# Dilated keys of a sample batch held once, new keys in the near tiles, page numbers read ahead

## The reference

```
for win, dil in DIL_CONFIGS:
    j = jnp.arange(win // dil + 1)
    idx = n_buf + jnp.arange(Tn)[:, None] - j[None] * dil
    g = kv_all[:, jnp.maximum(idx, 0)]
    s = jnp.einsum('bqhd,bqjhd->bhqj', q, g[:, :, :, 0]).astype(jnp.float32) * SCALE
    s = s - slopes[:, None, None] * (j * dil).astype(jnp.float32)
    p, lse = _masked_softmax(s, idx >= 0)
    outs.append(jnp.einsum('bhqj,bqjhd->bqhd', p.astype(q.dtype), g[:, :, :, 1]))
    lses.append(jnp.transpose(lse, (0, 2, 1)))
return _combine_dilations(outs, lses)
```

## Time and profile before

| | |
|---|---|
| median of 3 runs | 2328.37 us (2328.33 to 2331.82) |
| profiled execution | 2330.11 us, span 2328.2 us, mean granted TensorE clock 0.994 |
| TensorE matmul busy | 2238.4 us, 96% of the span |
| TensorE weight load busy | 1599.4 us, 69% |
| VectorE, ScalarE, GpSimd busy | 897.8 (39%), 566.9 (24%), 646.7 us (28%) |
| chain that ended last | PE 89%, DVE 4%, issue 4% |
| DMA | 448.19 MB, 193 GB/s on average |
| DMA's busy share, 465 to 582 us | 0.82 at 292 GB/s |

### The profile page before, as it was taken

The page is one execution under the profiler, slowest core; times in us unless marked ns, Lnnn a source line. Parts: engine busy times, 40 slices in busy tenths (PEclk is TensorE's granted clock), DMA queues, the critical chain, the costliest instruction groups (busy, mean ns, idle before and its releaser), DMA issues.

```text
span 2328.2 us, 43538 instructions
## 1 busy us (share of the span) xinstructions
PE 2238.4 (96%) x13592; PEld 1599.4 (69%) x13592; DVE 897.8 (39%) x2384; ACT 566.9 (24%) x1356; POOL 646.7 (28%) x719
## 2 busy tenths in 40 slices
PE   7999999999999999999999999999999899999998
PEld 4545567676766777777745455777676677777776
DVE  2013754343344222336510157434344522233374
ACT  2102651111123412220211046311111233221202
POOL 0002760101043443444100047410102424343340
PEclk9999999999999999999999999999999999999999
DMA  9633017888864444454375410388878545444441
GB/s 355 247 140 96 1 55 272 310 287 297 295 253 155 183 168 169 174 204 181 116 271 199 150 48 0 141 305 284 307 283 292 224 152 185 171 185 169 168 169 41
DMA packets 128818, 448.19 MB, mean 193 GB/s; under 512 B 17953, under 2 KB 89890, under 8 KB 107554
## 3 DMA queue, kind: packets, MB, share of 16 engines
q1 hardware_dynamic: 118768, 416.45, 48.8%
q10 hardware_dynamic: 9906, 29.98, 3.7%
HBM read 435.76 MB, written 152.57 MB: 253 GB/s over the span
## 4 chain that ended last, share of the span: by engine, by line
PE 89%; DVE 4%; issue 4%; POOL 1%; ACT 1%; DMA 1%; DVEq 0%; SPq 0%; POOLq 0%; ACTq 0%
PE bank L1062 39%; PE bank L1145 14%; PE bank L1358 10%; PE bank L1426 3%; PE bank L1534 3%; PE bank L1293 2%; PE bank L1325 2%; PE bank L1305 2%; PE bank L1158 1%; PE bank L1480 1%; PE bank L1559 1%; POOL zone L919 1%; PE bank L1506 1%; PE bank L1536 1%; PE bank L1543 1%
## 5 line engine op out<-in xcount | busy, mean ns | idle before, releaser
L1062 PE MATMUL bank<-zone,ring 128*128 128x288 f32 x1664 | 424.8, 407 | 9.0 <-DVE zone L1697 6.4
L1062 PEld LDWEIGHTS bank<-zone,ring 128*128 128x128 f32 x1664 | 314.8, 190 | 102.0 <-DVE zone L1697 11.8
L1062 PE MATMUL bank<-zone,w 128*128 128x288 f32 x1408 | 353.5, 406 | 0.0
L1145 PE MATMUL bank<-ring,hT 128*128 128x512 f32 (+2 forms) x800 | 330.1, 566 | 6.5 <-ACTq L749 5.0
L1062 PEld LDWEIGHTS bank<-zone,w 128*128 128x128 f32 x1408 | 267.5, 190 | 73.9
L1145 PEld LDWEIGHTS bank<-ring,hT 128*128 128x128 f32 (+1 forms) x800 | 147.5, 189 | 158.2 <-issue 147.1
L873 POOL TENSOR_TENSOR w<-ring 128x512 f32<-128x512 f32 x72 | 95.5, 1327 | 544.3 <-PE bank L1062 309.4
L1358 PE MATMUL bank<-ring,w 128*128 128x128 f32 x2048 | 242.5, 277 | 0.0
L1358 PEld LDWEIGHTS bank<-ring,w 128*128 128x128 f32 x2048 | 233.0, 192 | 4.0 <-issue 3.8
L611 ACT COPY zone<-bank 128x288 f32<-128x288 f32 x72 | 28.7, 398 | 559.8 <-PE bank L1062 559.8
L986 POOL TENSOR_TENSOR zone<-constants,stat 128x1024 f32<-128x1024 f32 x16 | 30.3, 1896 | 455.2 <-DVE stat L2056 455.2
(11 more groups left out here) (256 smaller groups left out, 2768.9 us busy)
## 6 DMA issues: line engine op xcount, KB each, us to landing
out_dil_s<-in_state_kv_dil SPq DMA_DIRECT2D x48, 2720.0 KB, 12.1
ring<-in_w_units SPq DMA_DIRECT2D x72, 1024.0 KB, 4.8
zone<-in_dilated_v SPq DMA_DIRECT2D x16, 3072.0 KB, 12.3
ring<-in_cache_kv_cmp SPq DMA_DIRECT2D x256, 128.0 KB, 2.2
ring<-in_cache_kv_sel SPq DMA_DIRECT2D x256, 128.0 KB, 6.3
ring<-in_w_in SPq DMA_DIRECT2D x10, 2048.0 KB, 8.1
zone<-in_dilated_k SPq DMA_DIRECT2D x16, 1280.0 KB, 5.8
zone<-in_dilated_k SPq DMA_DIRECT2D x16, 1024.0 KB, 7.9
```

Source lines behind the costliest of these rows:

```text
L1062: last = mm(dst[:, 0:HALF], lhs[:, k, :], rhs(k), start=first and k == 0, stop=(k == 3), skip_group_check=True)
L1145: last = mm(dst, hT[:, k, t * P:t * P + ROWS[t]], ring[:, n % 2, k * CH:k * CH + width], start=start and k == 0, stop=stop and k == KT - 1)
```

## The change

The dilated keys are held once. The last 128 keys make one tile; the near class covers the 384 positions before them, 96 keys in each of four tiles, and each near tile has room for the batch's 8 new keys (K_NEAR = 104); the two far classes have 96 keys a tile. The bias constant holds the logarithm of each key's count. GpSimd copies the batch's new keys into the near tiles (`new_keys`), and TensorE's first dilated score waits for that copy (`kd_new`) instead of the key DMA. New values are read from the output tensor `dil_s` by a DMA, to partitions 96 to 103 of the four near value tiles. So TensorE's products against new keys (L1460) and new values (L1536) go, and one of four transposes. Keys, values and window rows lie in one DRAM array, piece by piece; values come in four DMAs instead of two, of which those with 11 and 1 tiles fill 96 partitions.

The compressed values are computed ahead of the importance product, and ScalarE copies them earlier. VectorE forms the selected branch's new scores after `gs`. ScalarE copies the three transposed pieces one by one, and each value class waits for its own. The copy of the sample's new values by GpSimd at the projection's end goes.

The sync engine's loop is written out for seven batches. Page numbers of batch b+2 are read after the raw pages of b+1 are issued; those of batch 1 before the loop.

```diff
-SC_KTC, SC_S, SC_NEW, SC_WIN, SC_IMP, SC_SEL, SC_VC, SC_LEAST, SC_SUM, SC_OUT, SC_N = 0, 1, 2, 3, 4, 5, 7, 8, 9, 10, 11
+SC_KTC, SC_S, SC_NEW, SC_WIN, SC_VC, SC_IMP, SC_SEL, SC_LEAST, SC_SUM, SC_OUT, SC_N = 0, 1, 2, 3, 4, 5, 6, 8, 9, 10, 11
...
+NEAR, FAR = 96, 96
+K_NEAR = NEAR + NS
+AT_NEAR, AT_FAR = P, P + K_NEAR
+KEYS_D = AT_FAR + FAR
+KA, KB = 4 * P + 16 * K_NEAR, 16 * FAR
...
+    step = np.arange(FAR)[None]
+    dd = np.concatenate([PAST + td - (PAST - P + k), PAST + td - (PAST - WIN + 4 * step + td % 4), td - np.arange(NS)[None],
+                         PAST - 16 * step + 0 * td], 1)
+    nn = ((dd >= 0) & (dd <= 128)).astype(int) + ((dd >= 0) & (dd <= 512) & (dd % 4 == 0)) + ((dd >= 0) & (dd % 16 == 0))
+    nn[:, AT_FAR:] *= ~void
+    c["b_dil"] = np.where(nn > 0, -sd * dd + np.log(np.maximum(nn, 1)), NEG).astype(f)
...
-        kda, kdb = part(6656, ND_A, CH), part(9216, 4, CH)
+        kda, kdb = part(6656, KA), part(6656 + KA, KB)
+        kd_last, kd_near = part(6656, 4, P), part(6656 + 4 * P, 4, 4, K_NEAR)
+        kd_far = [part(6656 + KA, 4, 4, FAR), part(6656, 4, 4, FAR)]
...
+                    keys = of_batch("dilated_k", b, P)
+                    sp.dma_start(kda, keys[:, 0:KA]).then_inc(kda_ld.sem, 16)
+                    sp.dma_start(kdb, keys[:, KA:KA + KB]).then_inc(kdb_ld.sem, 16)
+
+                def load_dilated_v(b):
+                    sp.dma_start(vd[:, 0, :], of_batch("dilated_v_last", b, P)).then_inc(vd_ld.sem, 16)
+                    sp.dma_start(vd[0:NEAR, 1:ND_TILES - 1, :].rearrange("p g f -> p (g f)"),
+                                 of_batch("dilated_v", b, NEAR)[:, 0:(ND_TILES - 2) * CH]).then_inc(vd_ld.sem, 16)
+                    new = o["dil_s"][L, ds(b, 1), PAST - NS:PAST, CH:2 * CH].rearrange("o q r f -> (o q r) f")
+                    sp.dma_start(vd[NEAR:K_NEAR, 1:5, :], new.unsqueeze(1).to_broadcast([NS, 4, CH])).then_inc(vd_ld.sem, 16)
+
+                def load_last_v(b):
+                    sp.dma_start(vd[0:NEAR, ND_TILES - 1, :], of_batch("dilated_v", b, NEAR)[:, (ND_TILES - 2) * CH:]).then_inc(
+                        vd_ld.sem, 16)
...
+                load_last_v(0)
+                page = page_numbers(1)
+                for b in range(NB - 1):
                     it = l * NB + b
-                    page = page_numbers(b + 1)
                     sp.wait_ge(h_full.sem, h_full.at(it, 2))
                     sp.sem_inc(waits_taken_sp, 1)
                     load_raw(page, range(NPG))
+                    later = page_numbers(b + 2) if b + 2 < NB else None
                     sp.wait_ge(td_full.sem, td_full.at(it, TD_SD + 1))
                     load_dilated_k(b + 1)
                     sp.wait_ge(win_pv.sem, win_pv.at(it, 1))
                     sp.wait_ge(od_full.sem, od_full.at(it, 1))
                     load_window(b + 1)
-                    load_dilated_v(b + 1, 0, ND_TILES - 1)
-                    load_dilated_v(b + 1, ND_TILES - 1, ND_TILES)
+                    load_dilated_v(b + 1)
+                    load_last_v(b + 1)
                     sp.wait_ge(oa_full.sem, oa_full.at(it, 1))
                     sp.sem_inc(waits_taken_sp, 1)
                     load_selected(page)
+                    page = later
...
+                    a, z = BATCH_ROWS["dilated_k"]
+                    act.dma_start(kda[:, 0:KB], i["batch_rows"][ds(l, 1), ds(b, 1), a:z].rearrange(
+                        "o q (p f) -> (o q p) f", p=P)[:, KA + KB:]).then_inc(kda_ld.sem, 16)
                     act.wait_ge(sc_full.sem, sc_full.at(it, SC_KTC + 1))
                     copy(ktc, bank[SC_BANK[SC_KTC]][:, 0:P]).then_inc(kv_act.sem, 1)
                     act.wait_ge(sc_used.sem, sc_used.at(it, U_S + 1))
                     probs(s_c, 1, low)
+                    act.wait_ge(sc_full.sem, sc_full.at(it, SC_VC + 1))
+                    copy(vc, bank[SC_BANK[SC_VC]][:, 0:P]).then_inc(kv_act.sem, 1)
...
-                    copy(ptd[:, 0:3, :].rearrange("p e r -> p (e r)"), B[:, 0:384])
-                    copy(ptd[0:64, 3, :], B[0:64, 384:512]).then_inc(ptk_act.sem, 1)
+                    for e, R in enumerate((P, K_NEAR, FAR)):
+                        copy(ptd[0:R, e, :], B[0:R, e * P:(e + 1) * P]).then_inc(ptk_act.sem, 1)
...
+                def new_keys(it, b):
+
+                    pool.wait_ge(s_pad.sem, s_pad.at(it, 1))
+                    pool.wait_ge(kda_ld.sem, kda_ld.at(it, 1))
+                    pool.sem_inc(waits_taken_pool, 1)
+                    nc.gpsimd.tensor_copy(kd_near[:, :, :, NEAR:K_NEAR],
+                                          knb[:, :, ds(b * NS, NS)].unsqueeze(1).to_broadcast([P, 4, 4, NS])).then_inc(
+                                              kd_new.sem, 1)
...
-                    pe.wait_ge(kda_ld.sem, kda_ld.at(it, 1))
+                    pe.wait_ge(kd_new.sem, kd_new.at(it, 1))
...
+                        keys = (kd_last[:, p], kd_near[:, g, p], kd_far[late][:, g, p])[e]
+                        a, z = (0, AT_NEAR, AT_FAR, KEYS_D)[e:e + 2]
+                        M, strip = (P if e == 0 else 32), (0 if e < 2 else 1 if late else 2)
                         at = p * P + 32 * g
-                        return mm(S[32 * g:32 * g + M, e * P:(e + 1) * P], strips[:, a, at:at + M],
-                                  tile[:, p * P:(p + 1) * P], start=(j == 0 and p == 0), stop=(late and p == 3),
-                                  skip_group_check=True)
+                        return mm(S[32 * g:32 * g + M, a:z], strips[:, strip, at:at + M], keys,
+                                  start=(j == 0 and p == 0), stop=(late and p == 3), skip_group_check=True)
...
-                    for p in range(4):
-                        mm(S[:, 384:448], strips[:, 0, p * P:(p + 1) * P], knb[:, p, :], start=False, stop=(p == 3),
-                           skip_group_check=True)
                     pe.wait_ge(win_ld.sem, win_ld.at(it, 1))
...
+                    B = bank[SC_BANK[SC_VC]]
+                    for k in range(2):
+                        last = mm(B[:, k * HD:(k + 1) * HD], hid[:, 1, k * P:(k + 1) * P], w2[:, 1, :],
+                                  start=(k == 0), stop=(k == 1), skip_group_check=True)
+                    last.then_inc(sc_full.sem, 1)
...
-                    for e in range(4):
-                        R = 64 if e == 3 else P
-                        last = tr(B[0:R, e * P:(e + 1) * P], s_d[:, e * P:e * P + R], ident[:])
+                    for e, (a, z) in enumerate(((0, AT_NEAR), (AT_NEAR, AT_FAR), (AT_FAR, KEYS_D))):
+                        last = tr(B[0:z - a, e * P:(e + 1) * P], s_d[:, a:z], ident[:])
                     last.then_inc(td_full.sem, 1)
 
-                    pe.wait_ge(vd_ld.sem, vd_ld.at(it, 2))
-                    pe.wait_ge(ptk_act.sem, ptk_act.at(it, 3))
-                    pe.sem_inc(waits_taken_pe, 1)
+                    pe.wait_ge(vd_ld.sem, vd_ld.at(it, 4))
                     for j in range(ND_TILES):
+                        if j in (0, 1, ND_A):
+                            pe.wait_ge(ptk_act.sem, ptk_act.at(it, 3 + (0, 1, ND_A).index(j)))
+                            pe.sem_inc(waits_taken_pe, 1)
                         if j == ND_A:
...
+                        at, K = 32 * g + (16 if late else 0), (P, K_NEAR, FAR)[e]
+                        last = mm(bank[7][32 * g:32 * g + M, :], ptd[0:K, e, at:at + M], vd[0:K, j, :], start=(j == 0),
+                                  stop=(j == ND_TILES - 1), skip_group_check=True)
+                    last.then_inc(od_full.sem, 1)
...
-                    new_scores(s_sel[low, PAST // 2:PAST // 2 + 64], B[low, 64:128], const["nb_newa"][low, new], sm[low, 18:19])
-                    new_scores(s_win[:, WIN:WIN + 64], B[high, 0:64], const["nb_newa"][high, new],
-                               sm[high, 23:24]).then_inc(sc_used.sem, 1)
+                    new_scores(s_win[:, WIN:WIN + 64], B[high, 0:64], const["nb_newa"][high, new], sm[high, 23:24])
                     dve.wait_ge(s_exp.sem, s_exp.at(it, EX_CMP))
                     step(V.reciprocal(sm[low, 8:9], stat[low, 28:29]))
                     V.tensor_scalar(gs[:], const["gsum"][:], sm[low, 8:9], None, ALU.mult).then_inc(s_gs.sem, 1)
+                    new_scores(s_sel[low, PAST // 2:PAST // 2 + 64], B[low, 64:128], const["nb_newa"][low, new],
+                               sm[low, 18:19]).then_inc(sc_used.sem, 1)
...
-                    negated(s_d[:, 0:384], B[:, 0:384], const["b_dil"][:], sm[:, 24:25])
-                    step(new_scores(s_d[:, 384:448], B[:, 384:448], const["nb_newd"][:, new], sm[:, 25:26]))
-                    V.tensor_reduce(stat[:, 26:27], sm[:, 24:26], X, ALU.min).then_inc(td_used.sem, 1)
+                    negated(s_d, B[:, 0:KEYS_D], const["b_dil"][:], stat[:, 26:27]).then_inc(td_used.sem, 1)
```

More of the change, by code:

```diff
@@ L93 @@
 ND_TILES, ND_A = 13, 5
-CH_L, CH_A, CH_S = 6, ROUNDS * 4, 13
+NEAR, FAR = 96, 96
[3 more added lines that the diff above has]
```

(45 more changed lines are left out.)

42 lines of the change are left out of this document (12 added, 30 removed).

## The result

The changed kernel takes 2350.5 us (median of 4 runs, 2347.6 to 2351.8), the kernel before 2329.9: a ratio of 1.0088, 95% interval 1.0075 to 1.0100. It is slower by 0.9%, clear of the noise; 2289 was forecast. The profiled execution has a span of 2349.9 us (2328.2 before).

A forecast was written before the change was run, and what follows sets the result against it. TensorE, nearly without gaps, was taken as the bound. Savings of 1.06 + 0.50 + 1.05 + 0.30 - 0.10 = 2.8 us over 16 batches give 45 us; 5 come back in second batches: 40 off the 2328.4 median, 2289 us, range 2275 to 2304.

The forecast's parts named there:

- Parts 1 and 2: TensorE without new-key products, reordered around the group sums: late class 1.06 us earlier, value product saves 1.05 us a batch.
- part 4: Narrower dilated scores on TensorE, 48 products losing 24 or 32 of 128 columns: 0.3 us saved a batch.
- Part 3: Transposed dilated weights copied in three pieces by ScalarE: 0.98 us instead of 1.48, a gain of 0.50 a batch.
- the cap of roughly half of it: Weight loads at columns / 1.2 ns would limit the narrower scores' saving to roughly half of 0.69 us a batch.
- Part 5: GpSimd's copy of new keys: 0.4 us, hidden in running batches, nothing net in a layer's first; extra waits 0.05 a batch.
- Part 6: Sync engine's new order: loads hidden in running batches, selected pages with 3.7 us to spare; second batches lose 2.5 us each.
- Its term for the values: Transfer time of the dilated values: 2.69 MB moving at 0.41 MB/us, ahead of the selected pages.
- Rival E: Values so slow, under half of 0.41 MB/us, that selected pages bind every batch; at a third some 2390 us; chance 0.04.
- rival A: Values' transfer to 96 partitions doesn't shrink: 1.9 us more, second batch waits 4.4 us, 2293 us; chance 0.11.
- The second term of part 6: Each layer's second batch waits for selected pages, its keys issued behind page numbers: 2.5 us, twice (0.5 to 5 each).
- the selected pages' 6.4 us: Time for the selected pages, 2.1 MB, to arrive after the values, taken from the profile before.
- Rival B: Late keys become the wait: 6.6 us instead of 5, TensorE waits 1 us in 14 batches, 2303 us; chance 0.10.

The follow-up runs named there:

- e9: Changed kernel with all value tiles on 128 partitions, new values laid over them later, and page numbers read last in a batch: 2289.3 us.
- e11: Changed kernel with all value tiles on 128 partitions and new values laid over them later, page numbers still ahead of the dilated keys: 2324.5 us.
- e2: Kernel before with only the sync engine's loop written out and its page numbers moved as in the change: 2344.1 us.
- e3: Kernel before with its large value transfer cut into two DMAs, partitions 0 to 95 and 96 to 127: 2428.9 us.
- e4: Kernel before with its large value transfer cut into two DMAs, partitions 0 to 63 and 64 to 127: 2440.6 us.
- e12: Changed kernel with values on 128 partitions, new values laid over them later, and page numbers read between dilated keys and values: 2301.3 us.

## Why the prediction was wrong

- Parts 1 and 2 were right. The window scores start at 3.45 us of the batch (571.41; forecast 3.85 without narrowing), the importance product at 5.30 with 0.21 us of wait, the selected scores at 5.79 (6.14). The late class starts at 8.03, as forecast (8.0), but not as forecast in kind: part 4's narrowing made it ready 0.3 us sooner, and a wait for its keys took that back.
- Part 3 was right: 579.67 to 580.66 is 0.99 us (0.98 forecast, 1.48 before), though the gap is 0.45 us where less than 0.4 was named as the sign. The selected weights' transposes come at 16.86 (17.02).
- Part 4 was sized low: the narrow classes take 0.17, 0.14 and 0.21 us less, 0.52 in all; 0.3 was taken, 0.69 the upper end, and the cap of roughly half of it, worked out from the weight loads, did not hold.
- Part 5 was right: GpSimd's copy took 0.29 us, and the first batch waits 2.9 instead of 2.6. The period is 36.47 where 36.4 was forecast, and 36.16 without the wait for late keys (e9 and e11 have batches of 36.10); the 0.2 us between is part 4's.
- **Part 6 failed.** Its term for the values, 2.69 MB at 0.41 MB/us, took the rate of a transfer to 128 partitions for one to 96, where 2.36 of the 2.69 MB go. Measured is 0.20 to 0.24, so this piece takes 10 to 12 us instead of 6, more than the 3.7 us to spare. Rival E named the condition, under half of 0.41, and gave it 0.04; rival A took the port rule's milder size. The condition was met, nearly. Its price, 2390, was too high: at a half and not a third of the rate, a batch that waited gives the next one time, so only 8 of 14 wait.
- The second term of part 6, 2.5 us in each layer's second batch, was placed rightly and sized wrongly: with values on 128 partitions it is 9.1 and 8.7 us (e11). The step that failed is the selected pages' 6.4 us behind the values. In e11 the values end near 399 (forecast 396.5, with fewer bytes) and the pages are there at 410.7, 12 us later. By the windows the DMA engines moved some 3.9 MB in that time; the pages are 2.1 MB and the late keys 0.79, so the rest, by estimate 1 MB, is the next batch's raw pages, issued from 404.6 on, which the prediction left out. How much of the delay these transfers cause and how much the held issue (16.3 us for 16 pages) was not told apart. In e2 the pages came at 411.5, hardly later, but TensorE wanted them at 407.8 instead of 401.6: some 3.4 us of that from its longer batch, 2.7 from its slow first one.
- The late keys took 7.1 us to land (median of 16, in the changed kernel), not "at most 5.0". Rival B's condition, 6.6 us, was met; it cost 4.8 us in four batches, not 1 us in 14.
- A wait's price was taken as its length. In the second batch 49.42 us is 36.16 + 11.33 + 1.9: behind each long wait the clock was at its lower level. In e11 a batch with 2.3 us of waits lost 8.9 us in this way.
- That e9 takes 2289.3 us, the forecast's very number, is luck: its undisturbed batches (36.10 us) gain more than the 2.8 us forecast, and it loses 6.6 us to raw pages where the forecast had 5 for the selected ones. (The forecast's own sum, 2328.4 less 40, gives 2288.)

The sum of the change over the kernel before, by the profiled executions: 16 x 3.1 = 50 us gained; 48.9 for selected pages and 4.8 for late keys lost; that leaves 4 us slower. The spans differ by 21.7, so some 17 are left. Each of the eight batches with a wait for selected pages is 1.4 to 2.6 us longer than 36.16 plus its wait, 14.6 in all; that is the clock's part. The last 3 us are not accounted for.

## What to carry to other kernels

A byte count is no price for a DMA: cutting a tile from 128 to 96 partitions saved a quarter of the bytes and made the transfer longer by more than half (2.36 MB at 0.21 against 3.15 at 0.44 MB/us). Where TensorE is at 96% and the DMA engines at 82%, a faster TensorE brings its deadlines forward for every load: set up the whole chain of issues, with the issuing engine's own time, before banking the gain. Price a wait by what the clock does behind it, too. And on an engine that issues DMAs, try work that depends on nothing (here reading numbers) behind all issues: of three places it cost least there, though raw pages then came 6.6 us late in sum.

## What the runs showed of the hardware

- Transfers from DRAM to 128 partitions moved at 411 to 442 GB/s in the windows shown, to 96 at 197 to 237, to 64 at 209, with the DMA engines' share at 0.92 to 1.11 in all cases.
- Issuing took longer while earlier transfers were still queued, and held up everything behind it on the issuing engine. Issuing 16 selected pages took the sync engine 9.2 to 10.8 us where it came some 4 us behind the values (the kernel before, e9), 16 us directly behind values on 128 partitions (e2, e11), and 20 to 23 us behind values on 96 or 64 (20.1 in the changed kernel, 21.0 in e3, 22.5 in e4; 15.6 in the changed kernel's next batch). Single issues took up to 4.2 us in the changed kernel and 10.7 in e4.
- After 11 us of idleness TensorE was at the lower clock level (granted 0.50) and stayed there for some 4 us of work; after 3 to 4 us too (a wait of 3.14 us, then selected scores in 3.24 us instead of 1.94). Behind a wait of 1.84 us (e11) and of 1.91 us (e12) it was granted 0.50 for 20 us, and the batch took 47 us instead of 36.1; behind one of 2.06 us in the changed kernel it was not (38.41 us, wait and all). The length of the wait alone doesn't tell.
- Reading a page number took 0.55 to 0.59 us with the batch known at build time (16 from 374.1 to 382.4 us, and from 416.8 to 425.6, in the changed kernel).
